# Four weight tiles move from the differential attention's steps into the second half of the sparse attention's

## The reference, cut to what matters

```
h = rmsnorm(x, attn_norm[l]);  proj = h @ w_in[l]
q_a, kv_a, g_a, q_b, k_b, v_b, uv_c = split(proj)
o_a = nsa_attention(...)      # sparse: compressed + selected + window, gated
o_b = diff_attention(q_b, k_b, v_b, ...)      # a = p1 - lam * p2, rmsnorm
o_c = chunked_sgu(uv_c, ...)                  # gelu(u) * mix(rmsnorm(gelu(v)))
gates = sigmoid(h @ w_merge[l] + b_merge[l])  # 3 x 1024
mixed = gates0 * (o_a @ w_branch_a) + gates1 * (o_b @ w_branch_b) + gates2 * (o_c @ w_branch_c)
x = x + mixed @ w_out[l]
```

## Time and profile before

| | |
|---|---|
| median of the runs | 2696.58 us |
| profiled execution: own time, span | 2703.62 us, 2702.0 us |
| PE busy | 2451.9 us (91%) |
| PE weight loads | 2198.0 us (81%) |
| DVE busy | 1662.1 us (62%) |
| ACT busy | 1214.4 us (45%) |
| mean granted PE clock | 0.946 of full |
| sparse attention, pass A, PE's steps | 1651.8 to 1738.3 us |
| differential attention, pass A | 1738.3 to 1808.1 us |
| the same, pass B | 2220.2 to 2304.1 and 2304.1 to 2373.9 us |

### The profile page before, as it was taken

The page is one execution under the profiler, slowest core; times in us unless marked ns, Lnnn a source line. Parts: engine busy times, 40 slices in busy tenths (PEclk is TensorE's granted clock), DMA queues, the critical chain, the costliest instruction groups (busy, mean ns, idle before and its releaser), DMA issues.

```text
span 2702.0 us, 43597 instructions
## 1 busy us (share of the span) xinstructions
PE 2451.9 (91%) x16380; PEld 2198.0 (81%) x16380; DVE 1662.1 (62%) x2378; ACT 1214.4 (45%) x1574; POOL 73.4 (3%) x141
## 2 busy tenths in 40 slices
PE   3998989979979989899799898989899889988998
PEld 2997978869968978788789787679799876888897
DVE  6876656656768776665565554445655555555654
ACT  3444455444444444554344454354444443454443
POOL 0100000000000000000000000000000000000000
PEclk9998989989999999999999987899999988989999
DMA  7775544436647764444345433134455331334452
GB/s 302 276 277 174 185 164 163 163 122 220 246 171 250 277 235 156 173 155 159 138 156 186 171 127 108 63 125 162 160 182 183 139 141 63 126 125 156 170 181 100
DMA packets 74141, 461.52 MB, mean 171 GB/s; under 512 B 8272, under 2 KB 8416, under 8 KB 27648
## 3 DMA queue, kind: packets, MB, share of 16 engines
q1 hardware_dynamic: 53424, 384.33, 39.8%
q0 software_dynamic: 19120, 70.43, 7.4%
q10 hardware_dynamic: 1440, 4.62, 0.4%
HBM read 458.30 MB, written 1.05 MB: 170 GB/s over the span
## 4 chain that ended last, share of the span: by engine, by line
PE 85%; DVE 6%; ACT 4%; issue 3%; DMA 1%; DVEq 1%; ACTq 0%; SPq 0%
PE ps L594 19%; PE ps L374 16%; PE ps L375 16%; PE ps L376 16%; PE ps L596 9%; PE ps L431 2%; PE ps L491 1%; PE ps L442 1%; PE ps L458 1%; DMA set_a<-in_ada 1%; PE ps L471 1%; PE ps L457 1%; ACT whi L937 1%; DVE wlo L1366 1%; DVE x L1451 1%
## 5 line engine op out<-in xcount | busy, mean ns | idle before, releaser
L1366 DVE TENSOR_TENSOR wlo<-raw,whi 128x2048 fp32r<-128x2048 f32 x360 | 824.4, 2291 | 321.1 <-ACT whi L937 301.4
L937 ACT ACTIVATE whi<-raw 128x2048 fp32r<-128x2048 f32 x360 | 687.5, 1910 | 295.4 <-PE ps L376 292.1
L594 PE MATMUL ps<-hx,whi 128*128 128x512 f32 x2112 | 764.7, 405 | 33.0 <-DVE hx L1439 27.6
L596 PE MATMUL ps<-hx,wlo 128*128 128x256 f32 x2112 | 597.8, 283 | 0.0
L374 PE MATMUL ps<-hx,whi 128*128 128x256 f32 x1680 | 504.1, 300 | 27.0 <-DVE hx L1583 14.5
L594 PEld LDWEIGHTS ps<-hx,whi 128*128 128x128 f32 x2112 | 400.7, 190 | 141.8 <-DVE hx L1439 38.4
L375 PE MATMUL ps<-hx,whi 128*128 128x256 f32 x1680 | 486.9, 290 | 0.0
L376 PE MATMUL ps<-hx,wlo 128*128 128x256 f32 x1680 | 486.2, 289 | 0.0
L374 PE MATMUL ps<-yhi,whi 128*128 128x256 f32 x1440 | 408.5, 284 | 0.0
L375 PE MATMUL ps<-ylo,whi 128*128 128x256 f32 x1440 | 407.5, 283 | 0.0
L376 PE MATMUL ps<-yhi,wlo 128*128 128x256 f32 x1440 | 407.3, 283 | 0.0
(11 more groups left out here) (245 smaller groups left out, 2602.5 us busy)
## 6 DMA issues: line engine op xcount, KB each, us to landing
raw<-in_w SPq DMA_DIRECT2D x360, 1024.0 KB, 4.8
adat<-in_ada POOLq DMA_DIRECT2D x128, 512.0 KB, 4.5
raw<-in_ada SPq DMA_DIRECT2D x4, 512.0 KB, 11.3
blk<-in_block POOLq DMA_DIRECT2D x2, 990.5 KB, 5.0
set_a<-in_ada SPq DMA_DIRECT2D x3, 512.0 KB, 25.1
raw<-in_ada ACTq DMA_DIRECT2D x2, 512.0 KB, 11.8
set_b<-in_ada ACTq DMA_DIRECT2D x2, 512.0 KB, 17.5
x<-in_x SPq DMA_DIRECT2D x1, 1024.0 KB, 18.6
```

The source lines that it names most:

```text
L594: mm(ps[:, bank + i, :].rearrange("p (a s) -> p a s", a=2), whi[:, slot, col:col + P], hx[:, :, k, :], start=(k == 0), stop=False)
L596: last = mm(ps[:, bank + i, 0:S], wlo[:, slot, col:col + P], hhi[:, k, :], start=False, stop=(k == KD - 1))
L937: A(whi[:, slot, :], raw[:, slot, :], ACT.Copy).then_inc(*T.counts("hi_ready"))
L1366: tt(wlo[:, slot, :], raw[:, slot, :], whi[:, slot, :].bitcast(F32), ALU.subtract)\
```

## The change

Each engine's `beside_nsa` and `beside_diff` change in the same way, and the host puts the tiles into the new order. The two tiles of u move into steps 11 and 13 of the sparse attention, and the first two merge gates into steps 15 and 17. The tiles of v move to steps 0 and 1 of the differential attention, the first branch tile to step 2, the second pair of gates to steps 3 and 5, the second branch tile to step 6. Steps 4, 7, 8 and 9 have no tile. The number of tiles, matmuls and loads stays the same.

```diff
@@ PE
-                    if s in (3, 5):
+                    if s in (3, 5, 11, 13):
                         project("features")
                     elif s in (7, 9):
                         project("tokens")
+                    elif s in (15, 17):
+                        merge_gate()
...
                 def beside_diff(s):
                     if s < 2:
-                        project("features")
-                    elif s < 4:
                         project("tokens")
-                    elif s < 10:
-                        if (s - 4) % 3 == 2:
-                            if s == 6:
-                                wait_bank6()
-                            merge_branch(0)
-                        else:
-                            merge_gate()
+                    elif s in (2, 6):
+                        if s == 2:
+                            wait_bank6()
+                        merge_branch(0)
+                    elif s in (3, 5):
+                        merge_gate()
@@ ACT
+                    elif s in (11, 13):
+                        tile_done()
+                        take(u_act[:, s - 11:s - 9, :])
+                    elif s in (15, 17):
+                        merge_step((s - 15) // 2, 0, 0)
...
-                        take(u_act[:, 2 * s:2 * s + 2, :])
-                    elif s < 4:
-                        tile_done()
-                        take(vg[:, :, (s - 2) * S:(s - 1) * S])
-                    elif s < 10:
-                        merge_step((s - 4) % 3, 0, (s - 4) // 3)
+                        take(vg[:, :, s * S:(s + 1) * S])
+                    elif s in (2, 3, 5, 6):
+                        merge_step({2: 2, 3: 0, 5: 1, 6: 2}[s], 0, int(s > 2))
@@ DVE
+                    elif s in (11, 13):
+                        tile_done(False)
+                        T.n["pj_out"] += 1
+                    elif s in (15, 17):
+                        merge_step((s - 15) // 2, 0, 0)
...
-                    if s < 4:
+                    if s < 2:
                         tile_done(False)
                         T.n["pj_out"] += 1
-                    elif s < 10:
-                        merge_step((s - 4) % 3, 0, (s - 4) // 3)
+                    elif s in (2, 3, 5, 6):
+                        merge_step({2: 2, 3: 0, 5: 1, 6: 2}[s], 0, int(s > 2))
@@ host, weight_tiles
-        for j in range(1, 10):
+        for j in range(1, 8):
             put(slab(w, 1304 + 256 * j))
+        for j in range(2):
+            put(slab(inp["w_merge_2"][l], 256 * j))
+        for j in range(8, 10):
+            put(slab(w, 1304 + 256 * j))
+        put(slab(inp["w_branch_a_2"][l], 0, 512))
         for b, name in enumerate(("w_branch_a_2", "w_branch_b_2", "w_branch_c_2")):
-            merge(inp["w_merge_2"][l], 0, inp[name][l], b)
+            merge(inp["w_merge_2"][l], 0, inp[name][l], b, (0, 1) if b else (1,))
```

More of the change, by code:

```diff
@@ L2085, in ffn, with merge @@
         down(NJ - 1)
-    def merge(gates, g0, branch, n_):
-        for half in range(2):
+    def merge(gates, g0, branch, n_, halves=(0, 1)):
+        for half in halves:
             put(slab(gates, g0 + n_ * D + 512 * half))
```

## The result

The change is slower: 2730.85 us median (2727.67 to 2732.71) against 2696.92 us. The ratio is 1.0115 with a 95% interval of 1.0097 to 1.0134; the two medians alone give 1.0126. I had forecast 2703 us and a range that ended at 2711.

A forecast was written before the change was run, and what follows sets the result against it. PE was taken as the bound, busy 91% of 2702.0 us. Worked +5.6 us plus +1.2 us for the clock gave +6.8 us, put on the median 2696.58 as 2703 us, range 2694 to 2711.

The forecast's parts named there:

- The clock in the new steps: Sparse attention's new tiles: the clock may fall just as step 11's tile starts; +1.2 us for both passes.
- keep a tile and their length: Differential attention: steps 0, 1, 2, 3, 5 and 6 still carry a tile and take as long as before.
- the worked +5.6: Both stretches, both passes: sparse growth less differential gain, net +2.0 us in pass A and +3.6 in pass B.
- the tile of step 11: Sparse attention's first new tile: may start at low clock, between nothing and +5.95 us; half of +1.24 taken per pass.
- Behind the differential attention the clock falls anyway: After the differential attention, before the merge: the clock falls with or without the change; no cost was added.
- the waits of step 17, the join and step 4: PE idle time after the change: 1.4 us in step 17, 2.9 at the join, 2.2 in differential step 4.
- The gain of holding the clock up in the small steps: Sparse attention's small matmuls at full clock give back 10.6 us in pass A and 9.0 in pass B.
- Rival 1: Sparse attention: clock falls before the tiles, six start low at 1.24 us each; +13 us, 2710 us, chance 0.18.
- Rival 2: Steps 17, 18 and unit 7: ACT's splits add no waits; -3.4 us, 2693 us, chance 0.10.
- Rival 3: Sparse stretches: low clock costs a factor 2 instead of 1.80; net +3 us, 2700 us, chance 0.10.

The follow-up runs named there:

- e5: The change with one-pass spare matmuls wherever PE waits in its two stretches, and spare matmuls at the norm sums; 2708.82 us, ratio 1.0034.
- e8: The change, but in sparse attention step 18 ACT copies the last pair before rounding the next tile; 2713.00 us, ratio 1.0053.
- e1: Kernel before with only the two tiles of u moved to sparse steps 11 and 13, differential steps 0 and 1 empty; 2694.37 us, ratio 0.9977.
- e6: Kernel before, no tile moved, with two one-pass spare matmuls in each of sparse attention steps 10 to 18; 2684.78 us, ratio 0.9946.
- e3: The change with five spare matmuls ahead of each of the second block's four norm sums and four behind; 2721.88 us, ratio 1.0073.
- e11: The change with eight one-pass spare matmuls (1.7 us) per pass in dense work of the third merge; 2729.99 us, ratio 1.0113.
- e4: Kernel before, no tile moved, with one spare matmul (1.05 us) in each of sparse attention steps 10 to 18; 2692.38 us, ratio 0.9964.
- e9: Kernel before with one one-pass spare matmul in each of sparse steps 10 to 18, and more where PE waits elsewhere; 2685.48 us, ratio 0.9943.
- e10: The change itself measured again, unaltered, on the same chip as the runs beside it; 2727.41 us, ratio 1.0099.

## Why the prediction was wrong

**The step that failed is "The clock in the new steps".** It priced the clock at +1.2 us, half a slow start for one tile a pass, and the sum beside it let steps 0, 1, 2, 3, 5 and 6 of the differential attention "keep a tile and their length". Against e5, where the clock never falls, the changed kernel's two stretches cost 2.9 + 4.7 = 7.6 us more in pass A and 4.4 + 6.2 = 10.6 in pass B: 18.2 us. The sums, the layers behind them and the end added 6.0 more, for which the prediction had no term at all. With the worked +5.6 and the -3.2 of the rest that is the 26.6 us of the spans.

- *I asked only about the tile of step 11.* Its price was fair as a row: 7.39 us against 5.95, +1.4 (+1.3 in pass B) where I took 0.6. But I had read the low clock as a trait of one place. More was lost at the places that the change emptied: a wait of 2.7 us at the join, 2.2 in step 4 and 3.0 in step 8, each with only small matmuls near it. The first tile of the differential attention took 7.43 us and 8.26 in pass B, step 5's 7.68 and 7.74, where 5.95 and 5.85 were counted. The tiles of step 15 took 6.86 and 6.69, and that of step 17 7.42 in pass B.
- *"Behind the differential attention the clock falls anyway"* took everything later to be unchanged. The sums went from 1.99 us to between 3.6 and 3.8 in both passes. In e8, with the same tiles and a join wait shorter by 1.7 us a pass, they take 1.99 again; in e1, which has no such wait, they are slow. So the sums don't hang on the emptied steps alone.
- *The waits and steps.* Right: the waits of step 17, the join and step 4 to 0.3 us, and each stretch to 0.1 us at full clock (e5). The gain of holding the clock up in the small steps was right too. The two spare matmuls of e6 lengthen a step from 2.12 to 2.79 us, 6.0 us for nine steps, and cover some 1.3 us of waits, so by my estimate its 24.8 us would be about 20 without them, 11 and 9.5 us below the kernel before; I had 10.6 and 9.0.
- *Rival 1* named the mechanism and the sign and gave +13 us, with a chance of 0.18. It counted six tiles of the sparse attention at 1.24 us, and was to decide once three of them start low. Four did start low or run partly low: those of steps 11 and 15, at +1.4 and +0.9 us in pass A and +1.3 and +0.7 in pass B. Those of step 13 didn't. It left out the differential attention, the sums and what follows them, which made up 17 of the 24 us. So its 2710 us was as far off as the end of the range.
- *Rival 2* (no waits from ACT's splits) fell: e8 shows the split behind 1.7 us of the join. *Rival 3*, the factor 2, isn't borne out: it would give back 1.4 us more in pass A's sparse stretch, some 47.5 us, and e5 measured 48.97 where the rows at full clock give 48.9.

The size of the result thus comes from two things. The first is the worked net loss of 5.6 us: in each pass the tiles covered 7.9 us of waits where they stood and brought 4.6 us of new ones, and the small matmuls at full clock give back only 10.6 and 9.0 us. The second is the low clock behind the new gaps: spare matmuls in these gaps took 18.2 us out of the two stretches (e5). What sets the clock at one given place isn't settled. The same wait was followed by a slow and by a full-clock tile (e3), and why the sums are slow in the change, e1 and e11 but not in the kernel before and e8 stays open. The Trainium skill, TensorE: Matmul & The Clock Gate, "What's actually happening", says that the throttled state is the default and activity releases it. The trace agrees: in e4, e6 and e9 a few spare matmuls among the small ones keep the clock at 1.00 where it was 0.5, though PE was busy 23.82 of 23.90 us there, too.

No version with moved tiles beats e6 and e9, which move none: 2684.78 and 2685.48 us, 0.5% below the kernel before.

## What to carry to other kernels

Before filling a slow stretch with work taken from a covered one, ask whether it is slow from waiting or from the clock; if it is the clock, 0.4 to 0.7 us of spare matmuls a step may be cheaper than the real work, which covers waits where it stands. Each step that is emptied must be priced twice: by the chain it uncovers, and by the clock of what follows. To tell the two apart, fill the new gaps with spare matmuls: what the time then is, is the cost of the chains alone.

## What the runs showed of the hardware

- One spare matmul, one pass over 512 columns, in each step of 1.2 to 3.8 us held the granted clock at 1.00 for 23.5 us (e9; it makes a step of 2.12 us 2.56 long), where the same small float32 matmuls alone ran at 0.50 for 23.9 us although PE was busy all the time.
- The small matmuls and transposes cost 1.80 times as much at 1.2 GHz as at 2.4 (8.80 us against 4.88), not twice as much.
- The same 3.17 us wait before a norm sum of eight matmuls was followed by 1.99 us at full clock in the kernel before and by 3.78 us in the change.
- Removing 1.7 us of waiting in each of two places (e8) made the kernel 14 us faster against e10 and 18 us against the first measurement of the change; the norm sum some 175 us behind each place took 1.99 us instead of 3.8.
